# One more weight slot, another expert order, an earlier third mix, and empty rows left out of the gather in a hybrid attention, S5 and mixture-of-experts block

## The reference, cut to what matters

```
x  = x + g1 * (concat[a, s] @ W_out)
h2 = rms_norm(x) * (1 + sc2) + sh2
logits = h2 @ router_w + router_b;  top 4 of 32, softmax over the 4
for each expert e, for its tokens:
    z   = h2[tok] @ mlp1_w[e] + mlp1_b[e]          # 1024 -> 2048
    act = clamped SwiGLU of z                      # 1024
    y   = act @ mlp2_w[e] + mlp2_b[e]              # 1024 -> 1024
x = x + g2 * sum over the 4 of gate * y
```

## Time and profile before

| what | us |
|---|---|
| three timed executions | 1756.40, 1764.86, 1767.21 |
| their median | 1764.86 |
| the profiled execution | 1758.43 |
| its span in the trace | 1756.7 |
| start of PE's expert loop in the trace | 533.25 |
| end of PE's last matmul with weights | 1719.7 |

### The profile page before, as it was taken

One profiled execution on the slowest core, in us unless ns is written; L12 is line 12 of the kernel. 1 busy time (PEld: TensorE's weight loads), 2 busy tenths in 40 slices (PEclk: granted clock), 3 DMA queues, 4 the chain that ended last, 5 costly groups with the idle time before them and its releaser, 6 DMA issues.

```text
span 1756.7 us, 48721 instructions
## 1 busy us (share of the span) xinstructions
PE 1481.8 (84%) x19899; PEld 832.5 (47%) x19899; DVE 776.8 (44%) x1872; ACT 302.8 (17%) x844; POOL 530.6 (30%) x532
## 2 busy tenths in 40 slices
PE   4899998689648999999898998988978978986781
PEld 2356554364335555555554545554544534542340
DVE  4857365453365444444443433433433423422225
ACT  4121265342101111111111111110101100100000
POOL 3085999108002323222232222222211212211110
PEclk9997999899868999998999999998988988987885
DMA  9442224763761704478869999999999999999997
GB/s 270 151 49 48 86 47 98 261 200 107 299 254 43 309 20 164 163 291 322 344 269 403 358 407 368 354 408 408 408 408 408 408 408 408 408 409 409 408 408 295
DMA packets 141907, 495.58 MB, mean 282 GB/s; under 512 B 20216, under 2 KB 24580, under 8 KB 137744
## 3 DMA queue, kind: packets, MB, share of 16 engines
q1 hardware_dynamic: 128960, 469.60, 70.9%
q0 software_dynamic: 8416, 19.33, 3.1%
q10 hardware_dynamic: 4432, 5.25, 0.9%
HBM read 474.18 MB, written 17.84 MB: 280 GB/s over the span
## 4 chain that ended last, share of the span: by engine, by line
PE 53%; DMA 22%; SPq 15%; DVE 5%; issue 2%; ACT 2%; POOL 0%; ACTq 0%; POOLq 0%; DVEq 0%
PE bank L1789 30%; DMA w_ring<-mlp_w 17%; SPq L422 14%; PE bank L1506 5%; PE bank L1669 3%; PE bank L1594 2%; DMA ada_slab<-ada_w 2%; PE bank L1498 2%; DMA ada_half<-ada_w 2%; PE bank L1808 1%; PE bank L1781 1%; PE bank L1603 1%; PE bank L1769 1%; DVE final_acc L1421 1%; PE bank L1698 1%
## 5 line engine op out<-in xcount | busy, mean ns | idle before, releaser
L1789 PE MATMUL bank<-w_ring,xs_T 128*32 128x256 f32 x10240 | 620.9, 394 | 67.7 <-DMA w_ring<-mlp_w 67.5
L1789 PEld LDWEIGHTS bank<-w_ring,xs_T 128*32 128x32 f32 x10240 | 330.0, 113 | 319.9 <-DMA w_ring<-mlp_w 108.6
L643 POOL DMA_INDIRECT xs<-h_rows,row_idx x82 | 189.3, 2309 | 847.7 <-DVE row_idx L1349 817.4
L1789 PE MATMUL bank<-w_ring,act_T 128*32 128x256 f32 x5120 | 338.2, 402 | 56.1 <-DMA w_ring<-mlp_w 55.9
L1789 PEld LDWEIGHTS bank<-w_ring,act_T 128*32 128x32 f32 x5120 | 154.3, 114 | 175.3 <-DMA w_ring<-mlp_w 55.7
L1367 DVE TENSOR_SCALAR glu<-bank 128x128 f32<-128x128 f32 x160 | 46.6, 291 | 402.9 <-PE bank L1789 402.9
L945 DVE TENSOR_TENSOR slot_onehot<-iota_slots,slots 128x2048 bf16<-128x2048 f32 x83 | 189.3, 2281 | 0.0
L922 ACT ACTIVATE sigmoid<-glu 128x128 f32<-128x128 f32 x160 | 48.9, 306 | 536.2 <-DVE glu L1367 466.9
L926 ACT ACTIVATE act_T<-bank 128x128 f32<-128x128 f32 x160 | 44.3, 277 | 518.1 <-PE bank L1808 518.1
L664 POOL DMA_INDIRECT ys_rows<-y_rows_sb,row_idx x80 | 82.3, 1029 | 144.2 <-DVE y_rows_sb L945 141.9
L1344 DVE TENSOR_REDUCE row_idx_f<-bank 128x1 f32<-128x2 f32 x82 | 13.0, 159 | 209.0 <-PE bank L1769 209.0
(11 more groups left out here) (336 smaller groups left out, 1534.6 us busy)
## 6 DMA issues: line engine op xcount, KB each, us to landing
w_ring<-mlp_w SPq DMA_DIRECT2D x384, 1024.0 KB
ada_half<-ada_w SPq DMA_DIRECT2D x16, 1024.0 KB, 5.0
dense_ring<-w_in SPq DMA_DIRECT2D x4, 2048.0 KB, 14.6
final_rows<-ys_rows SPq DMA_DIRECT2D x4, 2048.0 KB, 14.4
dense_ring<-ada_w SPq DMA_DIRECT2D x3, 2048.0 KB, 29.3
w_out<-w_out SPq DMA_DIRECT2D x2, 2048.0 KB, 10.6
x_all<-x SPq DMA_DIRECT2D x2, 1024.0 KB, 14.3
ada_slab<-ada_w SPq DMA_DIRECT2D x1, 2048.0 KB, 40.3
```

The source lines that it names most:

```text
L643: pool.indirect_dma_start(out=xs[:], out_offset=None, in_=h2_v, in_offset=bass.IndirectOffsetOnAxis(ap=idx[:, 0:1], axis=0), bounds_check= ...
L1789: last = mm(bk[BLK * j:BLK * j + BLK, 0:ZW], x(h0 + i), w[:, i, ZW * j:ZW * j + ZW], start=False, stop=(stop and i == 1))
```

## The change

`SLOTS` becomes 23. The new slot lies at 120 KiB, where the loop's small tiles were; those move to other places, and `final_x1` from 172 to 96 KiB. The load of `gate_quarters` (`g2q`), whose new place holds routing constants until then, moves in SP's order from before chunk 16 to after chunk 20, behind the wait for step 3 of `blocks_ready`.

Only expert 0 is fixed (`FIXED` = 1). The others are ranked the other way round, the smallest first, and alternate. The blocks of the 32 places become

The diff, cut:

```diff
+FIXED = 1
-SLOTS_KIB = (132, 140, 64, 72, 32, 40, 0, 8, 16, 24, 172, 180, 80, 88, 156, 164, 96, 104, 112, 48, 56, 148)
+SLOTS_KIB = (132, 140, 64, 72, 32, 40, 0, 8, 16, 24, 172, 180, 80, 88, 156, 164, 96, 104, 112, 48, 56, 148, 120)
...
             sp.wait_ge(s["x1_ready"], NT)
+            sp.wait_ge(s["blocks_ready"], 1)
+            expert = sp.value_load(eat[0:1, 1:2], min_val=0, max_val=E - 1)
             for n in range(12, 16):
-                chunk(n)
+                chunk(n, expert)
...
             sp.wait_ge(s["blocks_ready"], 3)
+            for j in range(TILES):
+                sp.dma_start(g2q[BLK * j:BLK * j + BLK], dram["mod_rows"][0, 3 * D + ZW * j:3 * D + ZW * j + ZW]
+                             .partition_broadcast(BLK)).then_inc(s["mod_loaded"], 16)
             for n in range(21, SLOTS):
...
-                ch(pool.memset(jc[BLK * j:BLK * j + BLK, 0:1], float(j)))
+                ch(pool.memset(jc[BLK * j:BLK * j + BLK, 0:1], UNUSED * TILES / TOPK + j))
...
+            pool.wait_ge(s["x1_ready"], NT)
+            ch(pool.memset(xs[:], 0.0))
...
-                                        bounds_check=last_token).then_inc(s["xs_loaded"], 16)
+                                        bounds_check=last_token, oob_is_err=False).then_inc(s["xs_loaded"], 16)
...
-                ch(tt(cmp, bc(R[7][:, 2:E], 1, n, [P, n, n]), bc(R[7][:, 2:E], 2, n, [P, n, n]), ALU.is_gt))
+                ch(tt(cmp, bc(R[7][:, FIXED:E], 1, n, [P, n, n]), bc(R[7][:, FIXED:E], 2, n, [P, n, n]), ALU.is_lt))
...
+                ch(tt(ordm[:], bc(posn[:], 1, E, [P, E, E]), bc(iotaE[:], 2, E, [P, E, E]), ALU.is_equal))
+                ch(tt(lessm[:], ordm[:], bc(iotaE[:], 1, E, [P, E, E]), ALU.mult))
+                ch(dve.tensor_reduce(eatf[:], lessm[:], AX.X, ALU.add))
+                dve.tensor_copy(eat[:], eatf[:]).then_inc(s["blocks_ready"], 1)
...
-                dve.tensor_reduce(idf[:, 0:1], bank[6][:, 0:2], AX.X, ALU.add).then_inc(s["idx_sum"], 1)
+                dve.tensor_reduce(idf[:, 0:1], bank[6][:, 0:3], AX.X, ALU.add).then_inc(s["idx_sum"], 1)
...
             mix(1)
+            mix(2)
             h2_turn(0)
-            mix(2)
+            mix(3)
             router(0)
             h2_turn(1)
-            mix(3)
             router(1)
```

More of the change, by code:

```diff
@@ L210, in program @@
         rw = pack("router_w", [P, KT, E])
+        tri = pack("tri", [P, P], BF16)
+        onb = pack("ones_bf", [P, P], BF16)
+        ones = pack("ones", [P, P])
         rb = pack("router_b", [P, E])
@@ L234, in program @@
         warm = pack("table_warm", [P, 2])
-        ones = pack("ones", [P, P])
         oh4 = at("onehot4", 148, [P, NT, TOPK, E])
@@ L243, in program @@
         lessm = at("order_less", 196, [P, E, E], BF16)
-        lin = at("lin", 120, [P, 2, GW])
-        actT = at("act_T", 121, [P, 2, AH, P])
-        glu = at("glu", 122, [P, 2, GW])
-        sg = at("sigmoid", 123, [P, 2, GW])
-        g2q = at("gate2_quarters", 124, [P, ZW])
+        lin = at("lin", 197, [P, 2, GW])
+        actT = at("act_T", 128, [P, 2, AH, P])
+        glu = at("glu", K0 + 0.5 + 0.0625, [P, 2, GW])
+        sg = at("sigmoid", K0 + 1.5 + 0.0625, [P, 2, GW])
+        g2q = at("gate2_quarters", 129, [P, ZW])
         bsrc = at("b_src", 172, [96, 3072])
@@ L256, in program @@
         xT = at("xs_T", 203, [P, XH, P])
-        iotab = at("iota_slots", K0 + 2.25, [P, P])
+        iotab = at("iota_slots", K0 + 2.75, [P, P])
         fing = at("final_rows", 0, [P, 16, D])
-        fx1 = at("final_x1", 172, [P, NT, D])
+        fx1 = at("final_x1", 96, [P, NT, D])
         facc = at("final_acc", 80, [P, NT, D])
@@ L439, in _ @@
             sp.wait_ge(s["x1_ready"], NT)
+            sp.wait_ge(s["blocks_ready"], 1)
+            expert = sp.value_load(eat[0:1, 1:2], min_val=0, max_val=E - 1)
             for n in range(12, 16):
-                chunk(n)
+                chunk(n, expert)
             sp.wait_ge(s["h2_tr"], NT)
             sp.wait_ge(s["h2_ready"], NT)
-            for j in range(TILES):
-                sp.dma_start(g2q[BLK * j:BLK * j + BLK], dram["mod_rows"][0, 3 * D + ZW * j:3 * D + ZW * j + ZW]
-                             .partition_broadcast(BLK)).then_inc(s["mod_loaded"], 16)
             sp.wait_ge(s["x1_stored"], 16 * NT)
@@ L450, in _ @@
             for n in range(16, 21):
-                chunk(n)
+                chunk(n, expert)
             sp.wait_ge(s["blocks_ready"], 3)
+            for j in range(TILES):
+                sp.dma_start(g2q[BLK * j:BLK * j + BLK], dram["mod_rows"][0, 3 * D + ZW * j:3 * D + ZW * j + ZW]
+                             .partition_broadcast(BLK)).then_inc(s["mod_loaded"], 16)
             for n in range(21, SLOTS):
-                chunk(n)
-            expert = None
+                chunk(n, expert)
             for n in range(SLOTS, E * CPE):
@@ L459, in _ @@
                     last_block = sp.value_load(nbi[0:1, E + e:E + e + 1], min_val=0, max_val=MAXB - 1)
-                if n >= 2 * CPE and n % CPE == 0:
+                if n % CPE == 0:
                     expert = sp.value_load(eat[0:1, n // CPE:n // CPE + 1], min_val=0, max_val=E - 1)
@@ L598, in _ @@
             for col, pat, mult in ((0, [[0, NT], [0, TOPK]], 4), (1, [[TOPK * P, NT], [0, TOPK]], 0),
-                                   (2, [[0, NT], [1, TOPK]], 0)):
+                                   (3, [[0, NT], [1, TOPK]], 0)):
                 ch(pool.iota(tokid[:, :, col].rearrange("p (t k) -> p t k", k=TOPK), pattern=pat, base=0,
                              channel_multiplier=mult, allow_small_or_imprecise_dtypes=True))
-            ch(pool.memset(tokid[:, :, 3:4], -UNUSED))
+            ch(pool.memset(tokid[:, :, 2:3], -UNUSED))
             ch.sync()
@@ L707, in _ @@
                                scale=sgn[:, 0:1]).then_inc(s["bx_ready"], 1)
-            act.wait_ge(s["af_psum"], 1)
+            act.wait_ge(s["pe_prep"], 3)
             act.activation(AF[:].rearrange("p a g -> p (a g)"), bank[1][:, 0:4 * DG], ACT.Identity).then_inc(s["af_ready"], 1)
@@ L911, in _ @@
             h2_out(3)
-            act.wait_ge(s["blocks_ready"], 2)
+            act.wait_ge(s["blocks_ready"], 3)
             n_blocks = act.value_load(nbi[0:1, E - 1:E], min_val=1, max_val=MAXB)
@@ L1229, in order_positions @@
                 dve.wait_ge(s["part_mm"], 1)
-                n = E - 2
+                n = E - FIXED
                 ch(dve.tensor_scalar(R[6], bank[7][:, 6 * E:7 * E], float(E), None, ALU.mult))
@@ L1313, in _ @@
             dve.tensor_reduce(dslot[:], prod[:], AX.X, ALU.add).then_inc(s["blocks_ready"], 1)
-            dve.wait_ge(s["blocks_ready"], 1)
+            dve.wait_ge(s["blocks_ready"], 2)
             dve.wait_ge(s["bias_ready"], 2)
@@ L1319, in block_ends @@
                 ch.free(tt(R[2], R[4], R[0], ALU.add))
-                ch.free(tt(lessm[:], ordm[:], bc(iotaE[:], 1, E, [P, E, E]), ALU.mult))
                 ch.sync()
@@ L1481, in _ @@
                 last = tr(bank[1][:, q * DG:(q + 1) * DG], quad[:, q].rearrange("p a b -> p (a b)"), ident[0:DG, 0:DG])
-            last.then_inc(s["af_psum"], 1)
+            last.then_inc(s["pe_prep"], 1)
             early_ada(2)
@@ L1818, in _ @@
             x_turn(1)
-            pe.wait_ge(s["blocks_ready"], 2)
+            pe.wait_ge(s["blocks_ready"], 3)
             start = 0
             for e in range(E):
-                if e == 2:
+                if e == FIXED:
                     pe.wait_ge(s["sel_ready"], 2)
```

24 lines of the change are left out of this document (9 added, 15 removed).

## The result

| what | before | changed |
|---|---|---|
| timed executions | 1756.40, 1757.36, 1764.86, 1767.21 | 1734.86, 1735.63, 1736.16, 1737.24 |
| median | 1761.11 | 1735.89 |
| span of the profiled execution | 1756.7 | 1735.5 |

The ratio is 0.9844, with a 95% interval of 0.9820 to 0.9868: the changed kernel is faster, by 25.2 us in the medians and by 21.2 us in the spans. 44.5 us were forecast. Timed once more, beside 11 executions of the kernel before (median 1763.9), the changed kernel had a median of 1734.9, 29.1 us less, so the gain is 25 to 29 us. The time lies in the predicted range, 19 us above the predicted one.

A forecast was written before the change was run, and what follows sets the result against it. Neither PE nor DMA alone bounds: small experts wait for weights, large ones idle DMA. Terms - 41.5 (order, slot, earlier start), - 4 (empty places), + 1 (gate load) sum to - 44.5; 1713.9 from the profiled execution, 1720.4 from the median, said 1717; range 1702 to 1740.

The forecast's parts named there:

- start of the loop: PE's first matmul of the expert loop: at about 523.8 us instead of 533.25, 9.4 us gained, 6 to 12 by the bounds.
- gate load, first block: Load of gate_quarters behind nine chunks, needed in the loop's first block of 14.9 us: costs 0 to 2 us, 1 taken.
- eight cycles, to expert 15's second block: Eight steps from one large expert to the next, each 42.2 us plus its further blocks, ending at 1182.7 us.
- 180 chunks: Weight chunks still missing at expert 15's second block: 2.676 us each, 481.7 us, landed by 1664.4.
- behind the last chunk, to PE's end: PE's work after the last weights land: 1.5 us plus 12.3 for the last expert's second block, ending at 1678.2.
- empty places: Gathers skip rows of empty places, 2.36 MB less on POOL's queue: 4 us gained, bounds 0 and 5.8.
- behind PE's end: Stages after PE's last matmul: 37 us of the span, unchanged, with final_x1 landing during the extra block.
- The slot: A 23rd ring slot saves one chunk's transfer, 2.57 us, in each of 8 steps between large experts: 20.6 us.
- one price: From a large expert's last block's start to the next large one's second block: 44.8 us before, 36.0 of it chunk transfers.
- rival (a): Added slot saves 2.57 us only once, because restarting transfers sets the wait between large experts: 18 us lost, 1735; chance 0.11.
- The lead-in: Stages before the expert loop: earlier mixes make h2 of the last tile 12.2 us earlier, PE's loop start 9.4 us earlier.
- Rival (b): Before the loop, h2's store, longer order_positions and chunks 12 to 20 cancel the 9.4 us gain: 1726; chance 0.13.
- Rival (d): In the loop, skipping gathers take POOL longer, so PE waits in some 45 blocks: up to 1803 us; chance 0.04.

## Why the prediction was right in sign and 19 us off

The sum was made against the span: 1712.2 forecast, 1735.5 measured, 23.3 us apart. By the steps of the prediction:

| step | forecast | measured | us off |
|---|---|---|---|
| start of the loop | 523.8 | 525.7 | + 1.9 |
| gate load, first block | + 1 | + 1.3 (16.2 for 14.9) | + 0.3 |
| eight cycles, to expert 15's second block | 42.2 each | 44.3 (the first 42.7) | + 14.9 |
| 180 chunks | 481.7 | 480.7 | - 1.0 |
| behind the last chunk, to PE's end | 13.8 | 15.2 | + 1.4 |
| empty places | - 4 | nothing seen | + 4 |
| behind PE's end | 37.0 | 38.8 | + 1.8 |

**The slot** is the term that was mis-sized: "With 23 slots 13 chunks are missing and the price is 44.8 - 2.57 = 42.2 us." The pattern and the places of the large experts were read rightly: second blocks followed at the forecast distances, but each some 2 us too long. The prediction's own sign that the slot step is wrong, 81 us for a cycle with 5 blocks, is what came: 911.85 - 832.00 = 79.9 and 994.11 - 911.85 = 82.3. What failed is the translation of a chunk fewer into 2.57 us. It took the whole price beyond 36.0 us to be fixed, and gave no row for the rate within a refill or for PE's clock at its end. Neither stayed the same. Against the kernel before, the price should have fallen by 2.57 us and fell by 0.5. Of the 2.1 us that are missing, 0.7 are the lower clock (1.4 us a cycle, 0.7 before) and 0.8 the slower refill (4.1 us, 3.3 before); the other 0.6 stay open. The two profiles of one kernel differ by 0.9 us in the price, 0.4 of it by the clock and 0.3 by the refill, so the balance can't be much finer. The "one price" of before was a mean as well. With the three second blocks that the earlier trace rows leaves out,

```profile
881.83 3.46 PE bank L1789 x64
...
1033.62 3.46 PE bank L1789 x64
...
1103.31 4.26 PE bank L1789 x64
```

its six prices are, step by step, 44.8, 43.7, 45.4, 45.1, 45.2 and 44.5.

**The range** held because it had been widened for the rivals. 1735.9 lies outside the forecast's own bounds, 1703 to 1731. It agrees with the 1735 of rival (a) by chance: the runs with 22 and 21 slots show that the slot doesn't pay only once. Nearly all the terms that were off were off to the same side.

**The lead-in** came as argued: by the rows, tile 2 at 465.24, h2 of the last tile at 493.2 (491.8 forecast), `choose(3)` at 503.28, the first gather landed in 7.6 us. From the first mix on it is 7.8 us shorter with the lower clock and 10.3 without. Rival (b), that nothing is gained, is wrong. The mixes' place alone is worth 13.8 us of it, more than was forecast for the whole, since it also covers for the list of experts, which now stands ahead of `choose(3)`.

**The gate load** took 10.4 to 12.3 us instead of 3.0, behind chunks 12 to 20 in SP's ring. The Trainium skill, DMA: Bandwidth & Descriptors, Queues, rings and completion order, has one ring on each engine for the DMAs of one issuing engine, and the trace agrees. By the balance with the block of before, which took 15.0 us, it costs 1.3 us, near the 1 forecast; against a block that doesn't wait it costs 2.5.

**The empty places** were priced by bytes, 4 us with a lower bound of 0, and it was the lower bound. Two pairs of medians with and without the skip lie 2.7 and 3.4 us apart, on the side of no skip, within the uncertainty. **Rival (d)** didn't happen: gathers take 2299 ns on POOL and land after 7.1 us in the median, as in the earlier trace rows.

**The end:** the extra block was forecast with 12.3 us; it costs 13.2 us at PE's end and 2.4 behind it. The 0.9 us above 12.3 are its first `up` at the lower clock (4.32 us on the chain, 3.46 at the full clock).

## What to carry to other kernels

One more buffer in a ring saves its transfer time per refill only if the refill runs at the steady rate, so look at GB/s within a refill, in steps of 2 us, before pricing it, and at the granted clock where the engine has waited for the last piece. In an order that alternates large and small pieces of work, look at the last place separately: what stands behind the last transfer should be the smallest piece. A small load behind megabytes on the same issuing engine takes the time of those megabytes, so it goes out ahead of them if any memory is free for it.
